# The S5 outputs of each part issued in two halves, in two successive dilated-attention steps, with the gelu one step later

## What is computed

```python
bu = einsum('gpc,bsgc->bsgp', b_bar, uf)            # inputs of each state
_, h = associative_scan(combine, (a, bu), axis=1)   # linear recurrence over tokens
y = real(einsum('gcp,bsgp->bsgc', c_t, h)) + d_skip * uf
y = gelu(y)
gl = y @ w_glu
y = gl[..., :S5_WIDTH] * sigmoid(gl[..., S5_WIDTH:])
```

## Time and profile before

| what | value |
|---|---|
| median of 3 runs | 3624.54 us |
| lowest and highest | 3620.9 and 3627.59 us |
| the profiled execution's own time | 3622.69 us |
| its span | 3620.8 us |
| its mean granted TensorE clock | 0.953 of full speed |
| TensorE matmuls busy | 3353.2 us, 93% of the span |
| VectorE, ScalarE, GpSimd busy | 59%, 36%, 36% |

### The profile page before, as it was taken

The page is one execution under the profiler, slowest core; times in us unless marked ns, Lnnn a source line. Parts: engine busy times, 40 slices in busy tenths (PEclk is TensorE's granted clock), DMA queues, the critical chain, the costliest instruction groups (busy, mean ns, idle before and its releaser), DMA issues. The chain is left out here.

```text
span 3620.8 us, 43846 instructions
## 1 busy us (share of the span) xinstructions
PE 3353.2 (93%) x16295; PEld 2679.6 (74%) x16295; DVE 2129.0 (59%) x3010; ACT 1296.4 (36%) x2264; POOL 1289.4 (36%) x1046
## 2 busy tenths in 40 slices
PE   5699999989899999969999999898889979999998
PEld 3577777777688888747888887785557758888886
DVE  5346664454977677885333544574556475555586
ACT  3523343144333334432223333342751233232344
POOL 4021212111655530125445445361525325454111
PEclk7799999989899999989999999879999999999999
DMA  8621112123233337314465343562024423332552
GB/s 254 226 57 52 45 57 97 49 91 119 71 103 107 96 114 267 88 58 139 117 127 125 112 140 128 171 190 64 31 81 146 163 93 102 105 108 93 202 185 96
DMA packets 343340, 422.66 MB, mean 117 GB/s; under 512 B 22006, under 2 KB 249794, under 8 KB 341578
## 3 DMA queue, kind: packets, MB, share of 16 engines
q1 hardware_dynamic: 336008, 396.03, 35.1%
q0 software_dynamic: 6400, 16.94, 1.7%
q10 hardware_dynamic: 722, 6.89, 0.5%
HBM read 296.16 MB, written 122.98 MB: 116 GB/s over the span
## 5 line engine op out<-in xcount | busy, mean ns | idle before, releaser
L2350 POOL TENSOR_TENSOR up_w_lo<-up_w_sum,up_w_hi 128x512 fp32r<-128x512 f32 x176 | 248.4, 1441 | 326.4 <-ACT up_w_hi L2326 324.6
L3368 POOL TENSOR_TENSOR px_w_lo<-px_w_sum,px_w_hi 128x512 fp32r<-128x512 f32 x138 | 195.6, 1447 | 295.2 <-ACT px_w_hi L3179 295.2
L2350 POOL TENSOR_TENSOR up_w_lo<-up_raw,up_w_hi 128x512 fp32r<-128x512 f32 x132 | 201.3, 1541 | 129.3 <-ACT up_w_hi L2326 129.3
L1926 ACT CAST down_hi<-down_room 128x1024 fp32r<-128x1024 f32 x154 | 161.0, 1051 | 210.8 <-PE ps L2206 138.6
L1930 DVE TENSOR_TENSOR down_lo<-down_room,down_hi 128x1024 fp32r<-128x1024 f32 x154 | 190.3, 1240 | 71.9 <-ACT down_hi L1926 70.4
L2326 ACT CAST up_w_hi<-up_w_sum 128x512 fp32r<-128x512 f32 x176 | 99.7, 614 | 323.5 <-DVE up_w_sum L2339 323.5
L768 PE MATMUL ps<-h_hi,stream_hi 128*128 128x512 f32 (+1 forms) x488 | 185.3, 380 | 24.5 <-POOL stream_lo L743 17.2
L2556 PE MATMUL ps<-h_hi_at,up_w_lo 128*128 128x512 f32 x704 | 191.7, 395 | 15.9 <-POOL up_w_lo L2350 15.9
L2556 PE MATMUL ps<-h_hi_at,up_w_hi 128*128 128x512 f32 x704 | 192.9, 396 | 7.2 <-ACT up_w_hi L2326 7.2
L2556 PE MATMUL ps<-h_lo_at,up_w_hi 128*128 128x512 f32 x704 | 191.0, 394 | 0.0
L3179 ACT CAST px_w_hi<-px_w_sum 128x512 fp32r<-128x512 f32 x140 | 79.8, 616 | 306.6 <-DVE px_w_sum L3261 306.6
(11 more groups left out here) (608 smaller groups left out, 8203.1 us busy)
## 6 DMA issues: line engine op xcount, KB each, us to landing
up_raw<-in_w_up SPq DMA_DIRECT2D x88, 512.0 KB, 4.1
down_room<-hid_kept SPq DMA_DIRECT2D x154, 256.0 KB, 2.8
hid_kept<-up_out SPq DMA_DIRECT2D x44, 512.0 KB, 3.6
down_room<-in_w_down SPq DMA_DIRECT2D x88, 256.0 KB, 4.3
px_raw<-in_w_in SPq DMA_DIRECT2D x38, 512.0 KB, 5.2
proj_kept<-xT SPq DMA_DIRECT2D x34, 512.0 KB, 6.0
px_raw<-in_w_gate SPq DMA_DIRECT2D x32, 512.0 KB, 5.2
gates_kept<-xT SPq DMA_DIRECT2D x32, 512.0 KB, 6.0
```

Source lines behind the costliest of these rows:

```text
L1926: nc.scalar.copy(hi[:, u % R], both(u)).then_inc(hi_made, 1)
L2350: nc.gpsimd.tensor_tensor(w_lo[:, s, :], source(t, i), w_hi[:, s, :].bitcast(F32), ALU.subtract).then_inc(lo_made, 1)
L3368: nc.gpsimd.tensor_tensor(self.w_lo[:, s, :], self.source(t, i), self.w_hi[:, s, :].bitcast(F32), ALU.subtract).then_inc(self.lo_made, 1)
```

## The change

The function `outputs` takes a second argument. Half 0 holds the waits and the first two of four pairs of groups (12 matmuls), half 1 the other two pairs and the increment of `summed`. Half 0 is issued in the step in which all of it was before, half 1 in the next. Gelu is issued two steps after half 0, so at steps 11, 15, 19 and 23. Everything else stands where it was: the inputs of parts 2 and 3 are still issued at steps 11 and 15, and the first gated product at step 25.

```diff
--- before.py
+++ after.py
@@ -4346,13 +4346,14 @@
                                                 r.bm[:, j, q, 64 * gg:64 * gg + 64], r.chunk[:, 8 * m + 2 * q + gg, :], start=True, stop=True)
             last.then_inc(self.v_summed, 1)
 
-        def outputs(m):
-            pe.wait_ge(self.out_loaded[m], 16 * (S5_L + 1))
-            pe.wait_ge(self.s_ready, m + 1)
-            pe.wait_ge(self.x_made, 4 * min(m + 2, 4))
-            if m == 3:
-                pe.wait_ge(self.out, 3)
-            for q in range(4):
+        def outputs(m, half):
+            if half == 0:
+                pe.wait_ge(self.out_loaded[m], 16 * (S5_L + 1))
+                pe.wait_ge(self.s_ready, m + 1)
+                pe.wait_ge(self.x_made, 4 * min(m + 2, 4))
+                if m == 3:
+                    pe.wait_ge(self.out, 3)
+            for q in (2 * half, 2 * half + 1):
                 pair = [(2 * q + gg, slice(64 * gg, 64 * gg + 64), c.ps[:, gg, q * P:(q + 1) * P]) for gg in range(2)]
                 for g, rows, dst in pair:
                     nc.tensor.matmul(dst, r.toep[:, g, :], r.chunk[:, 8 * m + g, :], start=True, stop=False)
@@ -4360,7 +4361,8 @@
                     for g, rows, dst in pair:
                         last = nc.tensor.matmul(dst[:, 1:P], r.cp[rows, j, q, 1:POW, :].rearrange("p d ch -> p (d ch)"),
                                                 r.state[rows, j, q, 0:S5_N - 1], start=False, stop=(j == 1))
-            last.then_inc(self.summed, 1)
+            if half:
+                last.then_inc(self.summed, 1)
 
         def gate_rows(i, piece):
             t, n = divmod(i, 2)
@@ -4383,8 +4385,8 @@
             for m in range(4):
                 if step == self.at_in[m]:
                     inputs(m)
-                if step == self.at_out[m]:
-                    outputs(m)
+                if 0 <= step - self.at_out[m] < 2:
+                    outputs(m, step - self.at_out[m])
             for i, at in enumerate(self.at_glu):
                 if at <= step < at + 2:
                     gate_rows(i, step - at)
@@ -4449,7 +4451,7 @@
 
         for step in range(self.steps):
             for m in range(4):
-                if step == self.at_out[m] + 1:
+                if step == self.at_out[m] + 2:
                     gelu(m)
             for i, at in enumerate(self.at_glu):
                 if step == at + 2:
```

## The result

The changed kernel takes 3633.72 us (median of 6 runs, 3627.49 to 3637.63) against 3621.72 us for the kernel before (median of 6, 3615.5 to 3627.59). The ratio is 1.0031, with a 95% interval of 1.0018 to 1.0045, so it is slower by some 11 us. Its profiled execution took 3635.2 us with a span of 3633.1.

The account below looks back on a forecast made before the run. A loop from TensorE's outputs through gelu on ScalarE to GpSimd's store and next state was taken to bound the stage. Terms 6.7 + 5.3 - 2.0 = +10.0 us on 3624.5 gave 3634.5 us, range 3627.5 to 3641.5.

Parts of the forecast that it names:

- Part 0: Gelu one dilated step later delays GpSimd's store and next state, so outputs(1) start 4.1 us later; inputs(2) wait 2.1 us.
- Part 1: Gelu(1) and the next state move by 8.9 us; less 1.3 us of slack, outputs(2) start 7.6 us later.
- Part 2: Start of outputs(3): running sum +6.7 us, between +4.4 and +7.6, after 6.5 us of slack on GpSimd's path.
- the rival of the lost clock: Longer TensorE waits bring the low clock at outputs(2), costing about 3.9 us more: +13.9, 3638.4 us; chance 0.20.
- Part 3: Up to the gated product: gelu(3) 5.3 us later, less 2.0 for the second half at high clock, so +3.3 us.
- hidden up to the last step: Longer hand-offs of parts 0 to 2 are absorbed and only the last step counts: +3.3, 3627.8 us; chance 0.18.
- clock regained: Halves fill TensorE's idle time, low stretches run high, 14 us gained: -4, 3620.5 us; 0.06 with anything else below +0.
- What I said would show it: Gelu ends near 2372 and 2466; outputs(1) wait 3 to 4 us, gated product 8 or more; VectorE idles about 5.
- The hoped-for overlap: VectorE's idle time before the scores of step 22, behind outputs(3), should fall from 10.3 to about 5 us.
- One more sign: Stages before 2357 and after the barrier that closes the S5 stage should keep their lengths within 1 us.

Follow-up runs that it names:

- halves only: Outputs cut in two halves, gelu issued where it was, against the kernel before: 3626.24 us against 3623.8, ratio 1.0006; loop time 114.40 us.
- part 3 alone: Only part 3 split with its gelu later, parts 0 to 2 as in the kernel before: loop time 113.52 us, 3619.14 us in a single run.

## Why the prediction was right

The forecast was +10.0 us. The loop time rose by 10.1, the medians by 12.0, the ratio says 11. The direction, the size and the mechanism hold: a hand-off one dilated step later, passed on through GpSimd's queue. But of the terms of the sum two were off, +2.4 us in part 2 and -2.3 us in part 3, and that they cancelled is luck. The whole time came out near the forecast by a second piece of luck: 3633.72 us against 3634.5, from a kernel before that itself measured 3621.72 us in this comparison and not 3624.54.

- *Part 0*, +4.1: measured +3.9. Inputs(2) waited 1.97 us, forecast 2.1. What I missed is that the delay has two causes. I noted that the loads start 4.06 us later and then followed gelu alone. The experiment with halves only shows that the loads do it just as well without gelu.
- *Part 1*, +7.6: measured +7.9.
- *Part 2*, +6.7: measured +9.1. This term was mis-sized, above even the 7.6 that I gave as its upper end. I let GpSimd's slack of 6.5 us and TensorE's idle time take something back. Instead, outputs(2) ran at the low clock behind their wait of 2.83 us: the first half of outputs(2) takes 2421.33 - 2416.75 = 4.58 us, where that of outputs(0) took 2359.53 - 2356.98 = 2.55, and the step behind it 2425.83 - 2421.33 = 4.50 us. Gelu(2) came 19.07 us after the start of outputs(2), against 11.43 before. TensorE then stood idle for 6.39 us before outputs(3): GpSimd's last state operation ends at 2447.61 + 1.26 = 2448.87. On GpSimd's path the sum is 7.9 + (19.07 - 11.43) - 6.5 = 9.0 us: the longer hand-off was 7.6 us and not 5.65, and the slack was used up. This is the rival of the lost clock, true at outputs(2), though not for the whole amount that I gave it. That the longer wait caused the low clock is not shown. The length of a wait alone does not tell: in the kernel before, outputs(2) stayed high behind 1.31 us, and with the store moved the same outputs fell to the low clock behind 1.32 us (1.22 us for four matmuls from 2408.78).
- *Part 3*, +3.3: measured +1.0 from outputs(3) to the gated product, in the changed kernel and in the kernel with part 3 alone. The step between the halves took 2457.99 - 2453.46 = 4.53 us, not 5.33. And not only the second half ran at the high clock, as I had counted, but also the scores and transposes that gelu waits for. Before, those began at 2449.76 and still ran partly low: 1.92 us for the scores, against 1.16 at 2455.09. From the end of outputs(3) to gelu's table load it was 4.3 us before and is 2.7 us now.
- *The rival "hidden up to the last step"* (+3.3) is refuted in its form: parts 0 to 2 carried 8.8 of the 10.1 us.
- *The rival "clock regained"* did not happen as I had put it: the wait before outputs(1) grew, and they ran low. But from the second half of outputs(2) to outputs(3) the clock was 0.92 in place of 0.50. That gained nothing, since TensorE then waited for the state. With the store out of the way the clock made 8.2 of the 21.1 us.
- *What I said would show it.* Gelu(0) ended at 2371.28 and gelu(3) at 2465.45 (forecast 2372 and 2466, with the loop starting 0.8 us earlier). Outputs(1) waited 4.14 us (3 to 4). The gated product waited 6.67 us and not 8 or more. VectorE's wait before the scores of step 22 did not fall to 5 us:

```profile
DVE dil_lg L3616 <- PE ps L3556: 19.2, 5, 10.5
```

It is still 10.5 us, since TensorE's 6.39 us of idle time ahead of outputs(3) took the place of the half that had been moved away. The hoped-for overlap was eaten by the wait.

One more sign failed. I had said that the stages after the barrier keep their length within 1 us. From the next stage's first matmul to the end it is 1083.8 us before and 1086.8 us after. In the other kernels, which do not differ there either, it lies between 1082.8 and 1091.0 us, so 3 us are no more than the scatter between executions. With the loop's start 0.8 us earlier, they are why the two spans differ by 12.3 us and the loops by 10.1.

What stays open: how much of the clock's part is fixed by the code. In a single run with only part 0 split, outputs(3) ran at the high clock, in the kernel before at the low one, and the loop time came out shorter than before.

## What to carry to other kernels

When a piece of work is cut in two and its second half is moved behind other work, everything that waits for its *end* moves by the full length of that other work, not by half the piece. Follow every semaphore that is raised at the end, here one to the gelu and one to a loader, since undoing one of two parallel delays shows nothing. And see what an in-order queue does between two dependent operations: here a 4.2 us store with no dependant in the loop stood between, and moving it behind the state was worth 0.3% in the kernel before and took back all that the change had cost.

## What was not expected of the hardware

Besides the waits, the granted clock moved a good part of the time. TensorE was busy for all but 0.03 of 18.0 us after the wait of 4.14 us, and the granted clock was 0.53. The same kinds of matmuls, for the part before, ran from outputs(0) to outputs(1) at 1.00, across a wait of 1.97 us. Moving one store shortened the loop by 9 us in the kernel before and by 21 us in the changed one, and in both some 4 to 5 of 10 parts of it were busy time, not waits: the same matmuls took 95.6 us in place of 99.8, and 85.4 in place of 93.6.

The last row load took 5.5 us from its issue to its use with four weight loads of 256 KB and another row load just ahead of it, and 3.5 us with these issued before the store. Which of them made the difference was not tried apart.
